# Layer norms of a two-layer diffusion backbone: inverse deviation by square root and reciprocal in place of logarithm and exponential

## The reference, cut to what matters

```python
def _layer_norm(x, g, b):
    xf = x.astype(jnp.float32)
    mu = jnp.mean(xf, axis=-1, keepdims=True)
    var = jnp.mean(jnp.square(xf - mu), axis=-1, keepdims=True)
    return ((xf - mu) * lax.rsqrt(var + EPS) * g + b).astype(x.dtype)

x = _layer_norm(ALPHA * x + ml[2] * y_lat, ln_g[l, 0], ln_b[l, 0])
x = _layer_norm(ALPHA * x + ml[5] * _swiglu(_modulate(x, ml[3], ml[4]), ffn_w_in[l], ffn_w_out[l]),
                ln_g[l, 1], ln_b[l, 1])
```

## Time and profile before

| | us |
|---|---|
| median of 3 runs | 1930.9 (1926.65 to 1933.14) |
| the profiled execution's own time | 1919.39 |
| its span, first to last instruction | 1917.5 |
| PE busy | 1776.9 (93%) |
| POOL busy | 725.3 (38%) |
| DVE busy | 686.1 (36%) |
| ACT busy | 609.8 (32%) |

### The profile page before, as it was taken

One profiled execution on the slowest core, in us unless ns is written; L12 is line 12 of the kernel. 1 busy time (PEld: TensorE's weight loads), 2 busy tenths in 40 slices (PEclk: granted clock), 3 DMA queues, 4 the chain that ended last, 5 costly groups with the idle time before them and its releaser, 6 DMA issues.

```text
span 1917.5 us, 24418 instructions
## 1 busy us (share of the span) xinstructions
PE 1776.9 (93%) x9832; PEld 1428.5 (74%) x9832; DVE 686.1 (36%) x1183; ACT 609.8 (32%) x859; POOL 725.3 (38%) x381
## 2 busy tenths in 40 slices
PE   4999999999898999999999996989776999999996
PEld 2788766455587888888888874877565888888884
DVE  2134354566478311110111135830178761111114
ACT  0531322554435321121112224442233452222223
POOL 0442200265456422222322244533235854344443
PEclk8999999999999999999999997999888999999997
DMA  8412132354322212122212125212100323333221
GB/s 293 120 46 65 56 121 88 116 177 149 110 66 66 66 57 75 44 66 66 77 55 61 41 89 168 77 55 66 45 1 23 106 71 105 93 95 113 77 86 46
DMA packets 210265, 162.82 MB, mean 85 GB/s; under 512 B 17662, under 2 KB 190942, under 8 KB 210182
## 3 DMA queue, kind: packets, MB, share of 16 engines
q1 hardware_dynamic: 207744, 157.77, 27.4%
q10 hardware_dynamic: 2438, 3.90, 0.5%
HBM read 159.55 MB, written 2.10 MB: 84 GB/s over the span
## 4 chain that ended last, share of the span: by engine, by line
PE 79%; DVE 13%; ACT 3%; issue 3%; DMA 2%; POOL 1%; ACTq 0%; DVEq 0%; SPq 0%
PE ps L673 57%; PE ps L661 3%; PE ps L663 3%; PE ps L662 3%; PE ps L859 2%; PE ps L832 2%; PE ps L884 1%; DVE xT L1951 1%; PE ps L770 1%; PE ps L786 1%; PE ps L869 1%; DVE xT L1941 1%; DMA ring<-in_mod_w 1%; DVE cacc L2091 1%; PE ps L625 1%
## 5 line engine op out<-in xcount | busy, mean ns | idle before, releaser
L2300 POOL TENSOR_TENSOR wsplit<-ring,wsplit 128x1024 fp32r<-128x1024 f32 (+1 forms) x136 | 325.8, 2409 | 522.3 <-ACT wsplit L1436 522.1
L673 PE MATMUL ps<-hhi,wsplit 128*128 128x512 f32 (+1 forms) x1920 | 474.7, 355 | 6.3 <-DVE hu L1998 6.3
L673 PEld LDWEIGHTS ps<-hhi,wsplit 128*128 128x128 f32 x1920 | 317.2, 189 | 58.7 <-DVE hu L1998 6.9
L673 PE MATMUL ps<-hlo,wsplit 128*128 128x512 f32 x960 | 289.0, 355 | 0.0
L673 PE MATMUL ps<-uhi,wsplit 128*128 128x512 f32 x1008 | 250.7, 353 | 0.0
L1436 ACT ACTIVATE wsplit<-ring 128x1024 fp32r<-128x1024 f32 (+1 forms) x136 | 135.1, 1023 | 173.5 <-PE ps L673 173.5
L2048 DVE TENSOR_TENSOR hu<-sg,ps 128x768 f32<-128x768 f32 (+1 forms) x40 | 32.8, 821 | 439.4 <-ACT sg L1505 439.4
L673 PEld LDWEIGHTS ps<-uhi,wsplit 128*128 128x128 f32 x1008 | 165.8, 188 | 26.8
L673 PEld LDWEIGHTS ps<-hlo,wsplit 128*128 128x128 f32 x960 | 158.7, 189 | 25.9
L1914 DVE SCALAR_TENSOR_TENSOR xT<-ps,modc,xT 128x512 f32<-128x512 f32 x96 | 60.6, 659 | 275.7 <-PE ps L673 211.1
L673 PE MATMUL ps<-ulo,wsplit 128*128 128x512 f32 x504 | 151.0, 353 | 0.0
(11 more groups left out here) (334 smaller groups left out, 2720.7 us busy)
## 6 DMA issues: line engine op xcount, KB each, us to landing
ring<-in_mod_w SPq DMA_DIRECT2D x96, 512.0 KB, 4.7
ring<-in_ffn_w_in SPq DMA_DIRECT2D x88, 512.0 KB, 3.8
ring<-in_ffn_w_out SPq DMA_DIRECT2D x32, 512.0 KB, 4.1
ring<-in_m_w_in SPq DMA_DIRECT2D x24, 512.0 KB, 3.7
ring<-in_ab_w_in SPq DMA_DIRECT2D x21, 512.0 KB, 3.9
ring<-in_ffn_w_out SPq DMA_DIRECT2D x16, 384.0 KB, 3.4
ring<-in_ab_w_out SPq DMA_DIRECT2D x8, 512.0 KB, 4.2
ring<-in_m_w_out SPq DMA_DIRECT2D x8, 512.0 KB, 3.7
```

Of the source, the lines that this page charges most:

```text
L673: mm = pe.matmul(dst[:, a:b], w, h[:, a:b], start=st, stop=sp_)
L2300: pool.tensor_tensor(w_part(s, 1)[:, 0:width], ring[:, (NB[f"ffn{l}"] + s) % RING, 0:width], w_part(s, 0)[:, 0:width].bitcast(F32), ALU.su ...
```

## The change

Ahead of each norm the one-element activation is a square root. At the norm ACT takes the square root of `s2` in place and signals a new semaphore `ln_sd`. DVE, after its three leading centrings, waits for that, takes the reciprocal of the whole tile into `lnr`, signals `ln_rstd`, and waits for its own signal before the first multiplication.

```diff
+    ln_sd = sem("ln_sd")
...
         def layer_norm(i):
             l, nt = i // 2, NT[i // 2]
-            act.activation(lnr[:, 0:1], epsc[:, :], ACT.Ln)
+            act.activation(lnr[:, 0:1], epsc[:, :], ACT.Sqrt)
             act.wait_ge(ln_mm, 2 * i + 1)
             sums = ln_pairs(i)[0][:, 0:nt]
             act.activation(lnm[:, 0:nt], sums, ACT.Copy, scale=1.0 / D)
             act.activation(s1[:, 0:nt], sums, ACT.Square, scale=1.0 / D).then_inc(ln_mean, 1)
             act.wait_ge(ln_var, i + 1)
-            step(act.activation(lnr[:, 0:nt], s2[:, 0:nt], ACT.Ln))
-            act.activation(lnr[:, 0:nt], lnr[:, 0:nt], ACT.Exp, scale=-0.5).then_inc(ln_rstd, 1)
+            act.activation(s2[:, 0:nt], s2[:, 0:nt], ACT.Sqrt).then_inc(ln_sd, 1)
...
             for k in range(LEAD):
                 centre(k)
+            dve.wait_ge(ln_sd, i + 1)
+            dve.reciprocal(lnr[:, 0:nt], s2[:, 0:nt]).then_inc(ln_rstd, 1)
             dve.wait_ge(ln_rstd, i + 1)
```

## The result

| | before | changed |
|---|---|---|
| median, both run on one chip | 1926.65 us (9 runs, 1919.06 to 1933.14) | 1942.27 us (9 runs, 1938.51 to 1951.07) |
| ratio | | 1.0074, 95% interval 1.0054 to 1.0093 |
| profiled execution, its own time | 1919.39 us | 1938.51 us |
| its span | 1917.5 us | 1936.7 us |

The kernel is slower by 0.74%, 14.3 us at 1926.65, by the ratio on record; the two medians by themselves lie 15.6 us apart (0.81%).

What follows compares the result with a forecast made beforehand. PE was taken to set the pace, standing still for DVE at the norms, where added DVE time is mostly paid. 4.03 + 2.23 + 1.28 + 2.75 + 1.85 + 2.2 = 14.3 us takes the median from 1930.9 to 1945.2 us; range 1938 to 1957.

Steps and rivals of the forecast that it cites:

- The reciprocal: On DVE at all four norms: 158 ns fixed plus 5.0 ns an element, so 4.00 us at norms 0 and 1, 2.72 at 2 and 3.
- wide ones do not follow the slope of small ones: Sign of being wrong, at every norm: wide reciprocals off the 5.0 ns an element taken from 128x1 and 128x4.
- Norms 0 and 2: DVE's path to PE's start on `hu`: reciprocal and 0.03 us hand-over paid in full, +4.03 and +2.75 us.
- the delay breaks such a collision: Rival at norms 0 and 2: shifted DVE meets POOL otherwise, 2.2 us come back at each; +9.9 us, 1940.8 us, chance 0.06.
- Norm 1: PE's projection start moves from 1175.80 to 1178.03, waiting for DVE's modulation columns: +2.23 us.
- The first 1.8 us are covered by POOL: At norm 1 PE already waits for POOL's `wg`, so 1.8 us of DVE's 4.03 us delay cost nothing.
- can only come earlier: At norm 1 POOL's row starts from DMAs behind Exp on ACT, so it could only move earlier, by some 0.8 us.
- The gates: At ACT's L1582, behind norm 1, a load of Exp's table now stands ahead: +1.28 us, 0.1 less if it runs early.
- Norm 3: First multiplication at 1903.15 instead of 1901.30: +1.85 us, with ACT's shorter path worth 0.9 of the 2.75.
- The clock: PE's half-clock time after the waits of norms 0 and 2 grows: 1.1 us added to each, +2.2 us; ends 0 and some 5.
- ordinary rate: Rival at all norms: reciprocal costs no more an element than ordinary operations; +2.8 us, 1933.7 us, no measurable change, chance 0.08.
- eight passes: Rival at all norms: reciprocal at 8.2 ns an element, 6.4 and 4.3 us; +22.6 us, 1953.5 us; chance 0.24, or worse included.

## Why the prediction was right, and what was off in it

The forecast was +14.3 us and +0.74%; measured were 0.74%, and 15.6 us between the medians. The mechanism that was named, a reciprocal on the path that the others wait for, is shown at all four norms; at norm 1 it is only part of the loss. That the total agrees to the tenth of a per cent owes something to luck: the terms of the ledger sum to more than forecast, and the medians to less than the ledger.

**The reciprocal** was the term that was mis-sized: 5.0 ns an element from operations of 1 and 4 elements, 6.25 measured over 256 to 768. An error of 1 ns in a 178 ns operation is 0.25 ns an element at four elements. With 158 ns taken as fixed the slope came out at 5.0; with the 140 that the wide ones show, (178 - 140) / 4 is 9.5. So small reciprocals do not lie on the wide ones' line, which gives 165 ns at four elements, and the rows could bound the slope but not fix it. The prediction named this as a sign of being wrong, that wide ones do not follow the slope of small ones, and in size they did not. 6.25 is six times the 1.02 ns of the prediction's ordinary operation. The Trainium skill (VectorE: DVE Perf Modes, "Walkthrough: the 8-slice pipeline in each mode") has a repeat count of 8; an estimate by it was 6.4 and 4.3 us, and the trace has 4.94 and 3.34.

**Norms 0 and 2** were forecast at 4.03 and 2.75. They paid 5.59 and 4.04: the reciprocal and its hand-over 4.97 and 3.37, and 0.6 and 0.7 us for the collisions with POOL's splits. The rival in which the delay breaks such a collision had the sign wrong: DVE was held up a little more. In the kernel with norms 2 and 3 alone changed the same hold-ups stand at norm 2 as before, and it paid 3.34 us.

**Norm 1** is the step that failed: "The first 1.8 us are covered by POOL", with DVE's columns moving by the reciprocal alone. PE did start on L1707, as said, but DVE's columns came 6.45 us later and not 4.03 (from L1938 to their end 25.08 us before, 31.53 now): 4.97 for the reciprocal and 1.5 for two operations that read 1.78 and 1.47 us instead of 0.94, and a few that read 0.96 to 0.99. The cover was there, since 6.45 became 4.67, but what it covered had grown. The two stand beside POOL's cast and subtraction for `wg` (1169.20 to 1173.86). Before, POOL stretched instead: its four copies took 9.40 us, 3.31 now, and DVE's operations of this form beside them read 0.94 to 0.99.

The prediction also took ScalarE's shorter path at norm 1 for harmless: POOL's row "can only come earlier". It did come earlier, by 1.2 us behind L1938, and with the square root alone that cost 2.13 us, since DVE lost more beside POOL than before. The sizes are shown in ten traces. That POOL is what holds DVE up is read from the timelines; no run took POOL's preparation away, so that cause is argued, not shown, and so is which of the two loses in a given overlap.

**The gates** paid 1.20 us for the 1.28 us load, so it did run ahead of its activation, in the 0.1 us that the forecast allowed. No drain of the kind that the Trainium skill gives (ScalarE: Activation LUTs, "What ACT_TABLE_LOAD costs") is to be seen: the exponential starts at 1213.37, 0.01 us behind the load's end at 1213.36.

**Norm 3** paid 2.72, where 1.85 were forecast. The reciprocal is 0.62 longer than taken, and L1938 itself read 1.49 us instead of 1.24. Taking the exponential away saved 0.9 us of 3.62, as said.

**The clock** was taken at 2.2 us and cost about 1.5: 2.0 and 0.9 us more at half clock, of which half is lost.

The rival "ordinary rate" is excluded by 4.94 us, and the "eight passes" by the same line; its 1953.5 us lies beyond the ratio's interval.

## What to carry to other kernels

Before work is moved to another engine, look which engine the others wait for at that point. Here ScalarE had 1.1 us to spare at norms 0 and 1 and 0.2 at norm 2, and VectorE none. So 3.3 to 4.9 us of reciprocal were put on VectorE at each norm to take about 2 us off ScalarE, of which VectorE had waited for 0.83, at norm 3. Price an operation at the width at which it will run: a slope taken from operations of a few elements is mostly their fixed part. And when an engine's work shifts beside another's, earlier or later, add a term for the overlap that changes: 0 to 0.7 us at norms 0 and 2 here, 1.5 to 3.9 at norm 1. Look at it stage by stage, since a total with 10 us of scatter hides it.

## What the runs showed of the hardware

- A RECIPROCAL of fp32 from SBUF to SBUF on VectorE takes 0.14 us and 6.25 ns an element: 1.74, 2.54, 3.34 and 4.94 us at 256, 384, 512 and 768 elements. The second of two in a row reads 50 ns less (4.89 and 3.29).
- A VectorE TENSOR_TENSOR that begins right behind the start of a GpSimd subtraction of 128x1024 takes up to 2.2 us longer (0.94 becomes 3.16). In other overlaps it is GpSimd that stretches while VectorE's operations read 0.94 to 0.99 each: four small copies took from 0.76 to 9.40 us, one subtraction from 2.34 to 9.50. Which of the two loses is not told by the order of their starts: at norm 0 a subtraction starts 0.09 us ahead of a VectorE operation in both kernels (606.93 and 607.02 before, 610.71 and 610.80 now), and that operation reads 0.94 us before and 3.16 now. What decides it stays open.
- Beside a RECIPROCAL neither stretched: with two in a row, GpSimd's four copies (0.76 us) and its cast (1.04) ran beside the second one, which read 4.89 us.
- A table load starts before the semaphore of its activation is there, by 0.06 us in each of the four traces with this load (1212.08 against 1212.14 in the changed kernel).
- A part of the scatter between executions, up to 19 us for the kernel before, has nothing to do with the change. The first FFN runs at one of two rates, at a granted clock of 1.00 in both. PE's row for 640 to 1140 us, in the kernel before and in the one with the square root alone:

```profile
640.00:1140.00 500.00, 500.00 (x2887) 440.88 (x2886) 69.91 (x92) 96.14 (x107) 158.84 (x73) 1.00 0.22 63
```
```profile
640.00:1140.00 500.00, 500.00 (x2831) 433.61 (x2830) 67.08 (x89) 94.64 (x106) 154.36 (x71) 1.00 0.22 63
```

2887 matmuls against 2831 in the same time are 2%. From PE's start on `hu` to norm 1's L1938 five of the ten profiled executions took 525.1 to 526.3 us and five 534.9 to 535.9. The kernel before has 525.1 and the one with four centrings, which is the same up to norm 3, has 534.9, so it is not the code of this stretch. What sets it stays open. It is why a single pair of executions of this kernel can't tell 10 us. The ledger is of two executions at the same rate.
